# A first projection fed by a transposed copy of x, with its row scales taken later

## The reference

```python
def gmlp_mixer(h, w_in, ln_g, ln_b, ws, bs, w_out):
    z = h @ w_in                       # h = rms_norm(x, a_norm_g): 256 x 1024, w_in: 1024 x 6144
    u, v, g = jnp.split(z, 3, axis=-1) # 2048 columns each
    v = layer_norm(v, ln_g, ln_b)
    ...                                # v is mixed over the tokens of a chunk, giving sv
    y = u * sv * jax.nn.silu(g)
    return y @ w_out                   # added to x

first_block:  h = x + gmlp_mixer(rms_norm(x, a_norm_g), ...); then attention, then a final rms_norm
second_block: retention, then PEER experts; latent attention, then PEER experts again
```

## Time and profile before

| what | value |
|---|---|
| time, median of 3 runs | 2213.83 us (2212.69 to 2215.27) |
| profiled execution, its span from first to last instruction | 2211.2 us |
| the median of the runs less that span | 2.6 us |
| TensorE busy | 2188.4 us, 99% of the span |
| mean granted TensorE clock | 0.999 |
| VectorE, ScalarE, GpSimd busy | 70%, 55%, 51% |
| transfers | 398.98 MB, 180 GB/s in the mean |

### The profile page before, as it was taken

The page is one execution under the profiler, slowest core; times in us unless marked ns, Lnnn a source line. Parts: engine busy times, 40 slices in busy tenths (PEclk is TensorE's granted clock), DMA queues, the critical chain, the costliest instruction groups (busy, mean ns, idle before and its releaser), DMA issues.

```text
span 2211.2 us, 38524 instructions
## 1 busy us (share of the span) xinstructions
PE 2188.4 (99%) x12830; PEld 1914.8 (87%) x12830; DVE 1551.2 (70%) x3175; ACT 1218.6 (55%) x1831; POOL 1117.2 (51%) x491
## 2 busy tenths in 40 slices
PE   9999999999999999999999999999999999999998
PEld 7998989998888888888888889888888888888886
DVE  5523844435998888877777765499888887777777
ACT  5545644445568777744334346455787775333333
POOL 7978269587788777730000025678877774000000
PEclk9999999999999999999999999999999999999999
DMA  7645446356555555565556554555555555655653
GB/s 249 232 160 182 153 130 218 116 186 203 171 188 183 164 164 163 161 206 193 193 193 211 193 177 144 179 165 191 176 177 162 163 164 193 197 193 192 212 194 127
DMA packets 109930, 398.98 MB, mean 180 GB/s; under 512 B 12784, under 2 KB 13168, under 8 KB 109040
## 3 DMA queue, kind: packets, MB, share of 16 engines
q1 hardware_dynamic: 104832, 380.16, 52.7%
q10 hardware_dynamic: 4976, 17.17, 2.4%
HBM read 394.13 MB, written 3.15 MB: 180 GB/s over the span
## 4 chain that ended last, share of the span: by engine, by line
PE 83%; DVE 13%; issue 2%; ACT 1%; POOL 1%; DMA 0%; SPq 0%; DVEq 0%; POOLq 0%; ACTq 0%
PE GG L634 16%; PE XX L474 11%; PE XX L475 11%; PE XX L476 10%; PE GG L637 8%; PE GG L474 6%; PE GG L476 6%; PE GG L475 6%; DVE big L2194 2%; PE XX L945 1%; DVE big L2190 1%; DVE GG L2212 1%; PE XX L947 1%; PE GG L541 1%; DVE XX L2267 1%
## 5 line engine op out<-in xcount | busy, mean ns | idle before, releaser
L2526 POOL TENSOR_TENSOR w_lo<-ring,w_hi 128x1024 fp32r<-128x1024 f32 (+1 forms) x464 | 1106.7, 2404 | 735.4 <-ACT w_hi L1170 731.1
L1170 ACT ACTIVATE w_hi<-ring 128x1024 fp32r<-128x1024 f32 x722 | 757.7, 1056 | 599.0 <-PE XX L476 387.1
L634 PE MATMUL GG<-hT_both,w_hi 128*128 128x512 f32 x2208 | 560.4, 396 | 0.4 <-ACT big L1535 0.4
L634 PEld LDWEIGHTS GG<-hT_both,w_hi 128*128 128x128 f32 x2208 | 396.2, 189 | 71.6 <-ACT big L1535 0.9
L474 PE MATMUL XX<-w_hi,hT_both 128*128 128x512 f32 x1024 | 398.8, 389 | 1.8 <-DVE w_lo L2387 1.1
L476 PE MATMUL XX<-w_hi,hT_both 128*128 128x512 f32 x1024 | 398.4, 389 | 0.0
L475 PE MATMUL XX<-w_lo,hT_both 128*128 128x512 f32 x1024 | 398.4, 389 | 0.0
L2387 DVE TENSOR_TENSOR w_lo<-ring,w_hi 128x1024 fp32r<-128x1024 f32 x248 | 303.9, 1226 | 56.9 <-ACT w_hi L1170 56.8
L637 PEld LDWEIGHTS GG<-hT_both,w_lo 128*128 128x128 f32 x2208 | 301.2, 190 | 22.0
L637 PE MATMUL GG<-hT_both,w_lo 128*128 128x256 f32 x2208 | 307.5, 282 | 0.0
L474 PEld LDWEIGHTS XX<-w_hi,hT_both 128*128 128x128 f32 x1024 | 192.2, 188 | 43.4 <-DVE w_lo L2387 2.3
(11 more groups left out here) (329 smaller groups left out, 2825.8 us busy)
## 6 DMA issues: line engine op xcount, KB each, us to landing
ring<-slabs_in SPq DMA_DIRECT2D x722, 512.0 KB, 4.7
big<-rows_in ACTq DMA_DIRECT2D x10, 512.0 KB, 6.9
big<-rows_in ACTq DMA_DIRECT2D x3, 1024.0 KB, 6.9
big<-keys_in ACTq DMA_DIRECT2D x2, 1024.0 KB, 8.9
h_kept<-h ACTq DMA_DIRECT2D x2, 1024.0 KB, 12.6
h<-h_kept ACTq DMA_DIRECT2D x2, 1024.0 KB, 8.8
big<-ws_in ACTq DMA_DIRECT2D x1, 1024.0 KB, 7.8
out<-h SPq DMA_DIRECT2D x4, 256.0 KB, 2.0
```

What stands on the lines that cost most here:

```text
L634: nc.tensor.matmul(GG[pair][:, a, :], w_hi[:, q, w], hT_both[:, c, :, :].rearrange("p s t -> p (s t)"), start=c == 0, stop=False, skip_gro ...
L1170: nc.scalar.activation(w_hi[:, 2 * j + half, 0:n], ring[j][:, half * 1024:half * 1024 + n], ACT.Copy).then_inc(hi_ready, 1)
L2526: Q.tensor_tensor(w_lo[:, 2 * j + half, 0:n], ring[j][:, half * 1024:half * 1024 + n], w_hi[:, 2 * j + half, 0:n], ALU.subtract).then_inc( ...
```

## The change

x also arrives transposed (`xT_in`, chunk by chunk of 128 columns), and is loaded ahead of the slabs; the rows of x are loaded after the halves of slab 2. The first v groups use x times `a_g` without the row scale; the row scale is applied when a finished group is taken from its bank. The reciprocal roots are copied over 128 columns (`A_root`), transposed by TensorE after group 1, and multiply the transposed x on VectorE (`normed_columns`); ScalarE rounds the result (`round_normed`), VectorE makes its rest, and u and the gate use these.

```diff
# names and stages: "a_tr" becomes "a_root" (4 X tiles as before); A_g, of no use, goes; A_xT lies where xs lies
+        A_xT = area(0, DC, T)
+        A_root = area(8192, NB, P)
+        A_nh, A_nl = area_r("A_nh", 10240, DC, T), area_r("A_nl", 12288, DC, T)
# SyncE
-            sp.dma_start(h[:, 0, 0:512], x_in[0:P, 0:512]).then_inc(sem("x_loaded0_0"), 16)
+            load_columns(0, 2)                      # 256 KB of xT
             load(0, 0, slabs[0])
-            sp.dma_start(h[:, 1, 0:512], x_in[P:T, 0:512]).then_inc(sem("x_loaded1_0"), 16)
+            load_columns(2, 2)
             load(0, 1, slabs[0])
+            load_columns(4, 4)                      # 512 KB
             for half in range(2):
                 load(1, half, slabs[1])
-            with sp.Fori(1, N_SLABS // RING) as it:
+            for half in range(2):
+                sp.wait_ge(split_ready, half + 1)
+                load(0, half, slabs[2])
+                sp.dma_start(h[:, half, :], x_in[half * P:(half + 1) * P, :]).then_inc(sem(f"x_loaded{half}"), 16)
+            for half in range(2):
+                sp.wait_ge(split_ready, 2 + half + 1)
+                load(1, half, slabs[3])
+            with sp.Fori(2, N_SLABS // RING) as it:
# TensorE
+            def lead_columns(stage, src, rounded, rest):
+                hi, lo = src
+                for n in range(4):
+                    s, half = SLAB0[stage] + n // 2, n % 2
+                    ...
+                    pe.wait_ge(sem(rounded), n + 1)
+                    pe.wait_ge(hi_ready, 2 * s + half + 1)
+                    products(hi, w_hi, True, False)       # 4 matmuls of 512 columns
+                    pe.wait_ge(sem(rest), n + 1)
+                    products(lo, w_hi, False, False)
+                    half_ready(s, 0, half)
+                    products(hi, w_lo, False, True).then_inc(half_done, 1)
-            busy_at_start(15)
-            transpose_block("a_tr", xs, "xs_a", 0)
-            busy_at_start(2)
-            lead_wide("a_v", hT, ...)
-            project_wide("a_v", hT, first=1)
-            project_cols("a_u", hT, DC)
+            busy_at_start(9)
+            lead_columns("a_v", hT, "x_rounded", "x_rest")
+            def root_rows():
+                pe.wait_ge(sem("root_columns"), 1)
+                tile = x_begin("a_root", 0)
+                for b in range(NB):
+                    last = nc.tensor.transpose(tile[:, b * P:(b + 1) * P], A_root[:, b, :], ident[:, :])
+                last.then_inc(x_full, 4)
+            project_wide("a_v", hT, first=1, then={1: root_rows})     # called after group 1
+            nT = (A_nh, A_nl)
+            pe.wait_ge(sem("x_rest"), 8)
+            project_cols("a_u", nT, DC)                               # "a_g" with nT too
# ScalarE: the small transfers (positions, decay, invf) move behind the four splits; cols goes first
-            root_block("a", 0)
-            split_half(0, 0)
-            ...                                    # round_tile, split_half, root_block in turn
+            def round_columns(to, n):
+                for c in range(2 * n, 2 * n + 2):
+                    last = nc.scalar.activation(to[:, c, :], A_xT[:, c, :], ACT.Copy, scale=col("a_g", c))
+                last.then_inc(sem("x_rounded"), 1)
             act.wait_ge(sem("cols_loaded"), 16)
+            for n in range(4):
+                act.wait_ge(sem(f"xT_loaded{min(2 * n, 4)}"), 16)
+                round_columns(hT_hi, n)
+                split_half(n // 2, n % 2)
-            take_wide("a_v", A_v, (0,), {1: mix_weights, 4: first_row, 5: rotary_tables, 7: rates_and_row})
+            def round_normed():
+                for n in range(4):
+                    act.wait_ge(sem("x_normed"), n + 1)
+                    round_columns(A_nh, n)
+            split(RING)
+            split(1 + RING)
+            for b in range(NB):
+                root_block("a", b)
+            act.wait_ge(sem("root_columns"), 1)
+            take_v(0)                              # now with scale=rstd[:, 0:1]
+            mix_weights()
+            for j in range(2, 8):
+                if j % 2:
+                    take_v(j // 2)
+                split(j + RING)
+                if j == 4:
+                    first_row()
+                if j == 5:
+                    round_normed()
+                    rotary_tables()
+                if j == 7:
+                    rates_and_row()
# VectorE
+            def rest_columns(hi, lo, n, earlier):
+                dve.wait_ge(sem("x_rounded"), earlier + n + 1)
+                for c in range(2 * n, 2 * n + 2):
+                    last = V.scalar_tensor_tensor(lo[:, c, :], A_xT[:, c, :], col("a_g", c), hi[:, c, :], ALU.mult,
+                                                  ALU.subtract)
+                last.then_inc(sem("x_rest"), 1)
+            for n in range(4):
+                dve.wait_ge(sem(f"xT_loaded{min(2 * n, 4)}"), 16)
+                rest_columns(*hT, n, 0)
+                if n < 3:
+                    if n:
+                        dve.wait_ge(split_ready, n)
+                    rest_half(n // 2, n % 2)
             for b in range(NB):
+                dve.wait_ge(sem(f"x_loaded{b}"), 16)
                 ...                                # bn_stats of both halves
                 variance("a", b, False)
                 inverse_root("a", b)
-                ...                                # xs = h * rstd, and the rests of hT
+            V.tensor_copy(A_root, bc(rstd[:, 0:NB], 2, P)).then_inc(sem("root_columns"), 1)
+            def normed_columns():
+                tile, free = x_tile(dve, "a_root", 0)
+                for n in range(4):
+                    two = A_xT[:, 2 * n:2 * n + 2, :]
+                    V.tensor_tensor(two, two, bc(tile[:, 0:T], 1, 2), ALU.mult).then_inc(sem("x_normed"), 1)
+                ...
+                for n in range(4):
+                    rest_columns(A_nh, A_nl, n, 4)
             for g in range(4):
                 tile, free = w_tile(dve, "a_v", g, 1)
-                V.tensor_copy(A_v[:, 1, g * 512:(g + 1) * 512], tile[:, :]).then_inc(free, 1)
+                V.tensor_scalar(A_v[:, 1, g * 512:(g + 1) * 512], tile[:, :], rstd[:, 1:2], None, ALU.mult).then_inc(free, 1)
                 if g == 0:
                     turns_of_angles()
                 if g == 1:
+                    normed_columns()
                     angles_within_pi()
# GpSimd
-            pool.wait_ge(hi_ready, 1)
-            Q.tensor_tensor(w_lo[:, 0, :], ...)    # slab 0, half 0; then slab 1 on
-            split(1, 8)
+            pool.wait_ge(hi_ready, 4)
+            pool.wait_ge(split_ready, 3)
+            Q.tensor_tensor(w_lo[:, 3, :], ring[1][:, 1024:2048], w_hi[:, 3, :], ALU.subtract).then_inc(split_ready, 1)
+            split(2, 8)
```

More of the change, by code:

```diff
@@ L150, with build @@
 ROWN = dict(ROWS)
-def build(nc, h_kept, slabs, x_in, cols_in, rows_in, ws_in, keys_in, pos_row, pos_col, rope_in, diff_in, out):
+def build(nc, h_kept, slabs, x_in, xT_in, cols_in, rows_in, ws_in, keys_in, pos_row, pos_col, rope_in, diff_in, out):
     f32, u32, i32 = mybir.dt.float32, mybir.dt.uint32, mybir.dt.int32
@@ L488, in wide_half, with project_wide @@
                 return last
-            def project_wide(stage, src, ready=None, first=0, needed=lambda p, half: 2 * p + half + 1, following=None):
+            def project_wide(stage, src, ready=None, first=0, needed=lambda p, half: 2 * p + half + 1, following=None,
+                             then={}):
                 per, groups = WIDE[stage], SLABS[stage] // WIDE[stage]
@@ L506, in project_wide @@
                             wide_half(stage, g, p, half, src, range(NB)).then_inc(half_done, 1)
+                    if g in then:
+                        then[g]()
                     if tail:
@@ L609, in project_slab, with products @@
                     last.then_inc(half_done, 1)
+            def lead_columns(stage, src, rounded, rest):
+                hi, lo = src
+                for n in range(4):
+                    s, half = SLAB0[stage] + n // 2, n % 2
+                    q = 2 * (s % 2) + half
+                    parts = [(2 * n + i, b, slice(i * 512, (i + 1) * 512)) for i in range(2) for b in range(NB)]
+                    def products(x, w, start, stop):
+                        for c, b, part in parts:
+                            last = nc.tensor.matmul(G[wide_slab(stage, 0, b) % 4][:, :], x[:, c, b * P:(b + 1) * P],
+                                                    w[:, q, part], start=start and c == 0, stop=stop and c == DC - 1,
+                                                    skip_group_check=True)
+                        return last
+                    pe.wait_ge(sem(rounded), n + 1)
[5 more added lines that the diff above has]
+                    products(hi, w_lo, False, True).then_inc(half_done, 1)
             def lead_rows(stage, src, transpose_second, rounded, rest):
```

(20 more changed lines are left out.)

48 lines of the change are left out of this document (13 added, 35 removed).

## The result

The changed kernel takes 2221.03 us (median of 5 runs, 2220.71 to 2221.72) against 2213.14 (5 runs, 2212.69 to 2215.27): a ratio of 1.0033 [1.0022, 1.0044], slower by 0.3%. The profiled execution spans 2219.2 us, 8.0 more than before.

What follows compares the result with a forecast made beforehand. TensorE, 99% busy, was taken as the bound. u beginning 4.05 us later plus 2.5 for the clock made 6.55 on the span of 2211.2, 2217.7; with 2.6 around the span 2220.3, said as 2220; range 2212 to 2224.

Steps and rivals of the forecast that it cites:

- One number, the beginning of u: The whole change reduces to when u begins, 60.3 instead of 56.25, 4.05 us later, added to the end.
- The lead: At the start: first product at 7.1, group 1 begins at 18.7 instead of 23.6, 4.9 us gained; slow warm-up taken as 0.
- Group 2: Second v group: begins at 31.6 after TensorE waits 1.7 us for slab 4, ends at 42.5, 2.9 ahead of before.
- The chain from the end of group 2: Slab 7, copies, rests, angles, sines and slab 8 run in series for 17.8 us; TensorE waits 6.9 us ahead of u.
- my two sums: Rests of the normalized x end 10.0 us after group 2 if GpSimd holds VectorE, 6.9 us after it if not.
- The clock: TensorE's clock falls during the wait ahead of u, making u's first products slow; cost 2.5 us, bounds 0 and 2.5.
- The time around the span: The median of the runs stands 2.6 us above the profiled span; added to 2217.7.
- A: Rival: the wait at u without a fall of the clock; 2217.9 us, chance 0.17.
- B: Rival, not slower: GpSimd does not hold the rests, wait at u 3.8 us, clock kept; 2214.8 us, chance 0.15.
- D: Rival: the start's gain stays whole, slab 8 is ready in time, u begins at 51.7; 2209.2 us, chance 0.07.
- C: Rival: transfers of the first 20 us run at 300 GB/s, group 2 starts 2.6 us later; 2222.9 us, chance 0.11.

Runs made afterwards that it cites:

- experiment 1: The changed kernel, with VectorE making the angles ahead of normed_columns instead of behind it; 2216.27 us, ratio 1.0012.
- experiment 7: The changed kernel with the edits of experiment 4 and experiment 5 together; 2211.62 us, ratio 0.9991.
- experiment 3: The changed kernel, with the root's table loaded before the first copies, 12 warm-up products instead of 9, roots beside slab 3's halves; 2219.62 us.
- experiment 4: The changed kernel, with normalized x rounded one step earlier, sines one step later, angles between products and rests; 2220.94 us, ratio 1.0025.
- experiment 6: The changed kernel, with ScalarE's 1 MB row transfer moved from j = 4 to j = 6; 2219.07 us, ratio 1.0023.
- experiment 2: The changed kernel, with TensorE multiplying the identity 34 times ahead of its wait for u; 2219.16 us, ratio 1.0022.
- experiment 5: The changed kernel, with the normalized x written to PSUM banks instead of SBUF, order unaltered; 2219.67 us, ratio 1.0026.
- experiment 8: The changed kernel with the edits of experiment 3, experiment 4 and experiment 5 together; 2210.61 us, ratio 0.9993.
- experiment 9: Experiment 8 with rounding behind slab 5's split, rests ahead of angles, sines behind slab 9's split, decay logarithms behind slab 10's; 2213.67 us.
- experiment 10: Experiment 9 with the five row transfers issued one slab later and v's root one slab later; 2209.67 us, ratio 0.9982.

## Why the prediction was right

It said 2220 and the time is 2221.03; the mechanism it named, slab 8 behind a chain in series from the end of group 2, is the one that experiments 1 and 7 take away. That the number is so close is in part luck: u was put 2.3 us too early (60.3 for 62.56), the clock 0.8 too dear and the time around the span 0.8 too long, and these cancel to 0.7. The terms:

- **One number, the beginning of u.** Right: the balance closes within 0.3 us in all eleven kernels, if the clock and later waits of u are added.
- **The lead.** Mis-sized: group 1 at 20.57, not 18.7. The table load (4.52) comes only when the first piece of xT has landed, which I had not counted, so the first product is at 7.81 and not 7.1; and the first eight products took 3.75 us against 1.98 for eight later ones, the part for which I took 0 of 0 to 2.5 (the granted clock column says 1.00 here too). In experiment 3 both are gone. But slow first products are not in every execution: with the start of the change unaltered they took 3.67 to 3.75 us in experiments 1, 4 and 6, and 2.06 to 2.08 in 2, 5 and 7, though TensorE had stood idle 1.40 to 1.77 us ahead of them in both sorts. With the longer warm-up all four executions (3, 8, 9, 10) have 2.08 to 2.10; that the warm-up does it is likely, not shown. Experiment 2, with the start of the change:

```profile
8.06 2.08 PE L639 MATMUL GG<-w_hi,hT_both 128*128 128x512 f32 x8 [1.70 <-ACT w_hi L1214]
```

- **Group 2.** 32.45, not 31.6. Slab 3's second half was split from 22.47, not 21.0 (my own figures, 18.3 us from 1.9, end at 20.2 and not at 21.0); some 0.6 of that came back, most of it because the mixing weights are issued (28.11) while group 0 is taken and don't hold up slab 4's split. TensorE arrived 1.9 later than I thought and waited 0.62 instead of 1.7: as predicted, this wait hid the lead's error, here all of it. The transfers moved 324 GB/s up to slab 3, not 343 (window, last number):

```profile
1.90:22.40 20.50, 18.80 (x75) 15.92 (x76) 8.89 (x16) 12.01 (x16) 7.53 (x5) 1.00 0.91 324
```

- **The chain from the end of group 2 (about 43.4, predicted 42.5).** 19.15 us, not 17.8, and all of the difference is ahead of the angles. Slab 7's second half begins 4.8 behind that end, not 3.0: I let its 3.0 move with the end of group 2, but it waits for a transfer, and while group 2 ended 2.0 sooner, it came only 0.25 sooner (48.19 for 48.44; the row's transfer holds it, experiment 6). So GpSimd ends slab 7 at 51.73, 8.3 behind instead of 6.9; the first rest is held until then, the other seven follow freely, as predicted, and end 11.4 behind, not 10.0. From there on 7.8 us, as predicted. The eight copies take 3.29, not 2.6. That did not lengthen the chain, since the rests were held anyway, but it is one reason why the hold cost 1.5 (experiment 5) and not the 3.1 between my two sums (10.0 and 6.9).
- **The clock.** It fell, as taken; the price was 1.74, not 2.5 (experiment 2: 1.9).
- **The time around the span.** Predicted 2.6, here 2221.03 - 2219.2 = 1.8. The 2.6 set the median of three runs against the span of one execution that was not the median's; wherever time and span are of one execution, the kernel before's too, they differ by 1.7 to 1.9. This hid 0.8 of the 1.5 us by which the span was under-predicted.

The rivals: A fails with the fall of the clock. B fails twice: the first rest is held (and in experiment 4 all but the last), and where the hold is gone, in experiment 5, u still waits 6.33 us and the time is 2219.67, not 2214.8. D fails with u's long wait; what D priced, u at 51.7, needs another order than the change has, and in that of experiment 10 u comes at 52.84. C came in a mild form: 324 GB/s lies between 343 and its 300, and group 2 began 0.85 late, not 2.6.

## What to carry to other kernels

Where one engine is 99% busy, reduce a change near the start to the one moment from which the rest runs undisturbed, and add the clock. When you remove a stall, ask what that stall was keeping idle: GpSimd's pause made VectorE's rests fast, TensorE's lateness covered ScalarE's issuing, and each came up as the next wait (experiments 4, 8, 9) until its own step was moved. Before you reorder VectorE beside a busy GpSimd, put one of two SBUF operands in PSUM.

## What the runs showed of the hardware

- A VectorE instruction of two SBUF operands (128x256) beside GpSimd's stream cost 1.76 us on average (14.11 for eight, experiment 4), and 0.40 with one operand in PSUM (3.22 for eight, experiment 8).
- Not only two SBUF operands are held. The angles have a TENSOR_SCALAR with one tensor operand (128x320): in the kernel before it took 2.40 us beside GpSimd, in the change 0.33 while GpSimd stood idle:

```profile
41.78 2.40 DVE L1938 TENSOR_SCALAR big<-big 128x320 f32<-128x320 f32 x1
```

```profile
56.27 0.33 DVE L2035 TENSOR_SCALAR big<-big 128x320 f32<-128x320 f32 x1
```

- The clock fell to 0.50 with waits of 7.8 and of 3.5 us, and behind one of 2.50 (experiment 9), but not behind another of 2.48 (experiment 8, products 0.12 apart from the second on). Which of the two a short wait brings was not settled.
- What the clock cost did not go by the length of the wait: 2.75 us behind 3.5 (experiment 1), 1.74 behind 7.76.
